# Residual scaling behind tile 0's mixing, late modulation units between the first chunk's steps, and two more projection blocks as three single passes

## The reference, cut to what matters

```python
mod = silu(cvec) @ w_ada + b_ada                  # six rows of 1024, one set for prompt, one for sample
h = rmsnorm(x, g1) * (1.0 + sc1) + sh1
p = h @ w_in                                      # 2832 columns, for three groups of heads
mix = concatenate([fourier_mix(xa), conv_mix(xb), mlstm_mix(xc)])   # 256 + 256 + 512 = 1024 columns
x = x + ga1 * (mix @ w_out)
h = rmsnorm(x, g2) * (1.0 + sc2) + sh2
x = x + ga2 * moe(h, ...)                         # 16 experts in 4 groups, top 2 of one group
y = rmsnorm(x, final_g)
```

## Time and profile before

| | us |
|---|---|
| runs | 1074.56, 1075.64, 1080.11; median 1075.64 |
| the profiled execution | 1078.45, span 1076.5, mean granted clock 0.98 |
| busy: PE / PEld / DVE / ACT / POOL | 1010.8 / 800.5 / 671.7 / 431.6 / 204.2 |

### The profile page before, as it was taken

One profiled execution on the slowest core, in us unless ns is written; L12 is line 12 of the kernel. 1 busy time (PEld: TensorE's weight loads), 2 busy tenths in 40 slices (PEclk: granted clock), 3 DMA queues, 4 the chain that ended last, 5 costly groups with the idle time before them and its releaser, 6 DMA issues.

```text
span 1076.5 us, 18838 instructions
## 1 busy us (share of the span) xinstructions
PE 1010.8 (94%) x6265; PEld 800.5 (74%) x6266; DVE 671.7 (62%) x1121; ACT 431.6 (40%) x875; POOL 204.2 (19%) x240
## 2 busy tenths in 40 slices
PE   6899999989999999999959999988999999989997
PEld 3799999989999987799935666666566665656665
DVE  3444877147698823369955444677576766657677
ACT  3444222254322324679941222212454444344434
POOL 3010000000000001214650000001334433425314
PEclk9999999999999999999988999999999999989999
DMA  9953434313343322142361332257497888887956
GB/s 366 335 184 121 151 118 149 105 60 118 117 142 133 103 73 93 40 131 66 70 255 59 118 118 97 79 181 293 142 318 207 290 261 280 261 290 207 296 158 274
DMA packets 58301, 184.58 MB, mean 171 GB/s; under 512 B 7781, under 2 KB 20711, under 8 KB 52103
## 3 DMA queue, kind: packets, MB, share of 16 engines
q1 hardware_dynamic: 48920, 151.02, 39.5%
q0 software_dynamic: 7632, 27.79, 10.8%
q10 hardware_dynamic: 1696, 5.10, 1.2%
HBM read 149.73 MB, written 34.16 MB: 171 GB/s over the span
## 4 chain that ended last, share of the span: by engine, by line
PE 83%; DVE 5%; DMA 4%; ACT 4%; issue 2%; SPq 1%; POOL 0%; ACTq 0%; POOLq 0%; DVEq 0%
PE psum L1405 43%; PE psum L1347 31%; PE psum L1670 2%; DMA RB<-in_w_exp 1%; PE psum L1271 1%; DMA RW<-h_scratch,idxc 1%; DMA RB<-modrow_scratch 1%; PE psum L1287 1%; PE psum L1362 1%; PE psum L1570 1%; PE psum L1326 1%; DMA gvec<-in_gvec 1%; ACT RE L1152 1%; ACT RA L1162 1%; PE psum L1520 1%
## 5 line engine op out<-in xcount | busy, mean ns | idle before, releaser
L1347 PE MATMUL psum<-input_parts,weight_parts 128*128 128x320 f32 x2208 | 341.0, 313 | 3.0 <-DVE input_parts L1811 3.0
L1347 PEld LDWEIGHTS psum<-input_parts,weight_parts 128*128 128x128 f32 x2208 | 327.2, 190 | 11.8 <-issue 6.9
L1405 PE MATMUL psum<-RB,RW 128*128 x324 | 147.5, 606 | 8.4 <-DMA RB<-in_w_exp 4.8
L954 ACT ACTIVATE weight_parts<-RW 128x1024 fp32r<-128x1024 f32 x46 | 48.7, 1059 | 226.0 <-PE psum L1347 219.4
L1818 DVE TENSOR_TENSOR weight_parts<-RW,weight_parts 128x1024 fp32r<-128x1024 f32 x46 | 56.4, 1225 | 114.9 <-ACT weight_parts L954 114.7
L1405 PE MATMUL psum<-expert_parts 128*128 128x512 f32 x486 | 126.3, 413 | 1.1 <-DVE expert_parts L2343 1.1
L1405 PEld LDWEIGHTS psum<-RB,RW 128*128 128x128 f32 x324 | 60.7, 194 | 76.8 <-issue 76.6
L1405 PEld LDWEIGHTS psum<-expert_parts 128*128 128x128 f32 x486 | 91.3, 188 | 31.6 <-issue 14.3
L762 POOL TENSOR_TENSOR RE<-RE,RA 2x2304 f32<-2x2304 f32 (+1 forms) x2 | 9.1, 4529 | 353.7 <-DMA RA<-in_b_ada 353.6
L1405 PE MATMUL psum<-RC,RB 128*128 128x512 f32 x160 | 74.7, 612 | 0.0
L2362 DVE TENSOR_TENSOR expert_parts<-RB,expert_parts 128x1024 fp32r<-128x1024 f32 x54 | 63.8, 1223 | 9.2 <-ACT expert_parts L1219 8.0
(11 more groups left out here) (385 smaller groups left out, 1576.1 us busy)
## 6 DMA issues: line engine op xcount, KB each, us to landing
RB<-in_w_exp SPq DMA_DIRECT2D x48, 1024.0 KB
RW<-in_w_in SPq DMA_DIRECT2D x46, 512.0 KB, 4.2
RW<-in_w_ada SPq DMA_DIRECT2D x34, 512.0 KB, 3.4
RA<-in_w_ada SPq DMA_DIRECT2D x10, 512.0 KB, 13.9
RW<-gm_scratch SPq DMA_DIRECT2D x20, 256.0 KB, 3.4
h_scratch<-RE SPq DMA_DIRECT2D x10, 512.0 KB, 2.6
acc_scratch<-RA SPq DMA_DIRECT2D x10, 512.0 KB, 3.6
RB<-acc_scratch SPq DMA_DIRECT2D x10, 512.0 KB, 8.3
```

The source lines that it names most:

```text
L954: nc.scalar.activation(spl[:, r, 0], raw[:, r], ACT.Copy).then_inc(whi_ok, 1)
L1347: last = nc.tensor.matmul(psum[:, 2 * r + g, 0:GW], spl[:, r, wv, k], hT[:, xv, k, g * GW:(g + 1) * GW], start=(k == 0 and wv == 0 and xv ...
L1405: return nc.tensor.matmul(out, lhsT, rhs, start=start, stop=stop, **kw_)
```

## The change

Three parts change. `first_ada(2)` is issued ahead of step 1 of chunk 0, `first_ada(3)` ahead of step 2 and both `mod_columns` ahead of step 3; ScalarE copies their rows ahead of evictions 2 and 3. The two scalings of `A2` move behind `mix_tile(0)`, `mix_tile(1)`, the splits and the memsets, right ahead of the loop over tiles. For tiles 4 to 9 (`MORE = 4`) the blocks k 4 and 5 are three single passes too: ScalarE makes `heads_hi` (once) and `headp[..., 0]` (per tile), DVE `heads_lo` (in the place of w_out slices 4 and 5) and `headp[..., 1]`. `half_ps` gets one more count, after block 5 of tile 3, so that the slices are overwritten only when no float32 block needs them.

```diff
@@ -39,6 +39,7 @@
 SK = 2
 WARM = 3
 HK = 4
+MORE = 4
 LATE = 2
 HELD = (7, 9)
 LAG = 2
@@ -75,9 +76,13 @@
     RA = sbuf("RA", [P, 8 * T])
     RS = sbuf("RS", [P, 4 * D])
     RB = sbuf("RB", [P, NSLOT * T])
-    with nc.sbuf_tensor("row_of_slot", [P, LATE * T], F32R) as row_of_slot:
-        owner = row_of_slot[:, :].rearrange("p (b t) -> p b t", b=LATE)
+    with nc.sbuf_tensor("row_of_slot", [P, 5 * D], F32R) as row_of_slot:
+        owner = row_of_slot[:, 0:LATE * T].rearrange("p (b t) -> p b t", b=LATE)
+        heads_lo = row_of_slot[:, 0:2 * D].rearrange("p (k n) -> p k n", k=2)
+        headp = row_of_slot[:, 4 * D:5 * D].rearrange("p (b v k t) -> p b v k t", b=2, v=2, k=2)
     RC = sbuf("RC", [P, NT * NH * (HD + 1)])
+    with nc.sbuf_tensor("heads_weight", [P, 4 * D], F32R) as heads_weight:
+        heads_hi = heads_weight[:, :].rearrange("p (s b n) -> p s b n", s=2, b=2)[:, :, 0]
     RW = sbuf("RW", [P, 4 * D])
     RE = sbuf("RE", [P, 3 * T])
     rows1_ = sbuf("rows1", [P, P])
@@ -261,7 +266,7 @@
     assert mb + 4 * FE <= rb + 2 * D
     G_U = SK * 2 * FE
     D_U = KD * 2 * FE
-    SPLIT0 = 2 * NCH + HK + NT - 1
+    SPLIT0 = 2 * NCH + HK + NT - 1 + 2 + NT - MORE
     yb = RE[:, 0:2 * D].rearrange("p (b c) -> p b c", b=2)
     gmix, gmix_last = RC[:, 4 * D:5 * D], RC[:, LATE * T:LATE * T + D]
     token = RC[:, LATE * T:(LATE + 1) * T]
@@ -444,7 +449,10 @@
     STORED = 32 * (NT // 2)
 
     def mix_split(t):
-        return 2 * NCH + (1 if t == 1 else HK + t)
+        return 2 * NCH + (1 if t == 1 else HK + t if t <= MORE else HK + 2 * t - MORE + 2)
+
+    def heads_split(t):
+        return 2 * NCH + HK + 2 * t - MORE + 3
 
     def wout_split(k):
         return 2 * NCH + 2 + k
@@ -926,9 +934,9 @@
                 g = h * KD + k
                 if h == 0 and k == 0:
                     act.wait_ge(mod_ok, 3)
+                if h == 0 and k in (2, 3):
+                    first_rows(k)
                 if h == 0 and k == KD // 2:
-                    first_rows(2)
-                    first_rows(3)
                     act.wait_ge(mod_ok, 6)
                 act.wait_ge(tr_ps, g + 1)
                 if g >= 2:
@@ -1163,8 +1171,18 @@
                                          accum_out=hss[:, 0, ft, hd:hd + 1]).then_inc(hsq_ok, 1)
         def mix_high(t):
             h, cols = tile_cols(t)
-            act.wait_ge(half_ps, t)
+            act.wait_ge(half_ps, t if t <= MORE else t + 1)
             nc.scalar.activation(mixp[:, 0], PT[:, h, 0:HK, cols], ACT.Copy).then_inc(whi_ok, 1)
+
+        def heads_high(t):
+            h, cols = tile_cols(t)
+            if t == MORE:
+                act.wait_ge(mod_ok, 6 + 2)
+                act.wait_ge(h2_ok, 2 * PT_TILES)
+                for k in range(2):
+                    nc.scalar.activation(heads_hi[:, k], wout(HK + k), ACT.Copy).then_inc(whi_ok, 1)
+            act.wait_ge(mix_ok, NH * t + 2)
+            nc.scalar.activation(headp[:, t % 2, 0], PT[:, h, QQ:QQ + 2, cols], ACT.Copy).then_inc(whi_ok, 1)
 
         act.wait_ge(fn_ok, JOINED)
         act.wait_ge(hn_ok, NT)
@@ -1182,6 +1200,8 @@
                 nc.scalar.activation(score[:, 0:BATCH * NE], psum[:, 6, 0:BATCH * NE], ACT.Sigmoid).then_inc(sig_ok, 1)
             if t + 2 < NT:
                 mix_high(t + 2)
+                if t + 2 >= MORE:
+                    heads_high(t + 2)
             h2_transposed(t)
             logits_part(t)
         act.wait_ge(lg_ps, NT)
@@ -1334,9 +1354,9 @@
                     pe.wait_ge(cm_ev, ev)
                 for k in range(KD):
                     if first:
-                        if h == 0 and k == KD // 2:
-                            first_ada(2)
-                            first_ada(3)
+                        if h == 0 and k in (1, 2):
+                            first_ada(1 + k)
+                        if h == 0 and k == 3:
                             mod_columns(2, 2)
                             mod_columns(3, 2)
                         if k + 2 < KD:
@@ -1618,17 +1638,25 @@
                     pe.wait_ge(mix_ok, NH * (t + 1))
                 if k < HK and t >= 1 and g != 1:
                     pe.wait_ge(wlo_ok, wout_split(k) if t == 1 else mix_split(t))
+                if k == HK and t >= MORE and g != 1:
+                    pe.wait_ge(wlo_ok, heads_split(t))
+                if k < HK and t >= 1:
+                    parts = mixp[:, 0, k], mixp[:, 1, k], wout_hi[:, k], wout_lo[:, k]
+                elif HK <= k < HK + 2 and t >= MORE:
+                    parts = headp[:, t % 2, 0, k - HK], headp[:, t % 2, 1, k - HK], heads_hi[:, k - HK], heads_lo[:, k - HK]
+                else:
+                    parts = None
                 for half in range(2) if g is None else (g,):
                     out, c = psum[:, 2 * (t % 2) + half, :], slice(half * 512, (half + 1) * 512)
-                    if k < HK and t >= 1:
-                        mm(out, mixp[:, 0, k], wout_hi[:, k, c], k == 0, False)
-                        mm(out, mixp[:, 0, k], wout_lo[:, k, c], False, False)
+                    if parts:
+                        mm(out, parts[0], parts[2][:, c], k == 0, False)
+                        mm(out, parts[0], parts[3][:, c], False, False)
                     else:
                         last = mm(out, PT[:, h, MIX[k], cols], wout(k)[:, c], k == 0, k == KD - 1)
-                if k < HK and t >= 1:
+                if parts:
                     for half in range(2) if g is None else (g,):
-                        last = mm(psum[:, 2 * (t % 2) + half, :], mixp[:, 1, k], wout_hi[:, k, half * 512:(half + 1) * 512], False, False)
-                if k == HK - 1 and g is None:
+                        last = mm(psum[:, 2 * (t % 2) + half, :], parts[1], parts[2][:, half * 512:(half + 1) * 512], False, False)
+                if (k == HK - 1 or (k == HK + 1 and t == MORE - 1)) and g is None:
                     last.then_inc(half_ps, 1)
                 if k == KD - 1:
                     last.then_inc(o_ps, 1)
@@ -2099,14 +2127,20 @@
                                         hss[:, 2, ft].unsqueeze(2).broadcast_to([P, NH, HD]), ALU.mult).then_inc(hn_ok, 1)
 
 
-        dve.wait_ge(rows_b, 16 * 7)
-        for q in range(2):
-            nc.vector.scalar_tensor_tensor(A2[:, q], A2[:, q], 1.0, g2row, ALU.add, ALU.mult).then_inc(mod_ok, 1)
-
         def mix_low(t):
             h, cols = tile_cols(t)
             dve.wait_ge(whi_ok, mix_split(t))
             nc.vector.tensor_tensor(mixp[:, 1], PT[:, h, 0:HK, cols], mixp[:, 0].bitcast(F32), ALU.subtract).then_inc(wlo_ok, 1)
+
+        def heads_low(t):
+            h, cols = tile_cols(t)
+            if t == MORE:
+                dve.wait_ge(half_ps, MORE + 1)
+                dve.wait_ge(whi_ok, heads_split(t) - 1)
+                for k in range(2):
+                    nc.vector.tensor_tensor(heads_lo[:, k], wout(HK + k), heads_hi[:, k].bitcast(F32), ALU.subtract).then_inc(wlo_ok, 1)
+            dve.wait_ge(whi_ok, heads_split(t))
+            nc.vector.tensor_tensor(headp[:, t % 2, 1], PT[:, h, QQ:QQ + 2, cols], headp[:, t % 2, 0].bitcast(F32), ALU.subtract).then_inc(wlo_ok, 1)
 
         dve.wait_ge(so_ok, 2)
         mix_tile(0)
@@ -2183,6 +2217,9 @@
         dve.wait_ge(tab_in, 48)
 
 
+        dve.wait_ge(rows_b, 16 * 7)
+        for q in range(2):
+            nc.vector.scalar_tensor_tensor(A2[:, q], A2[:, q], 1.0, g2row, ALU.add, ALU.mult).then_inc(mod_ok, 1)
 
         def normed(t):
             q = 0 if t < PT_TILES else 1
@@ -2223,6 +2260,8 @@
             if t + 2 < NT:
                 mix_tile(t + 2)
                 mix_low(t + 2)
+                if t + 2 >= MORE:
+                    heads_low(t + 2)
             if t == BATCH:
                 dve.wait_ge(sig_ok, 1)
                 choose(0, BATCH, *pairs_a)
```

## The result

| | before | changed |
|---|---|---|
| timed together: median (lowest to highest) | 1076.40 us (1074.56 to 1080.11) | 1059.84 us (1057.69 to 1061.54) |
| ratio | | 0.9841 [0.9808, 0.9873] |
| timed again on another chip | 1080.86 us | 1058.93 us, ratio 0.9808 [0.9756, 0.9861] |
| the profiled execution, span | 1078.45, 1076.5 | 1059.77, 1058.0 |

What follows compares the result with a forecast made beforehand. TensorE was taken to bound the kernel, with 83% of the span in its chain. Gains of 11.5 + 3.3 + 2.6 = 17.4 us off 1078.45 gave 1061.0 profiled, median 1058.2 us; range 1055.0 to 1065.0.

Steps and rivals of the forecast that it cites:

- Part 1: Tile 0: moving the two scalings behind the mixing ends tile 0 11.5 us earlier; bounds 9.3 and 12.0.
- a walk's 12.0: Tile 0: step-by-step timing of TensorE and DVE gave 12.0 us; 11.5 taken, as meeting chains seldom meet exactly.
- The two chains: Tile 0's h2 ready at 574.0, just when TensorE asks for it at 574.0; the scalings' cover is used up.
- The clock: Rival: granted clock falls again in tile 0, the head or both; price 1.3 and 2.2, 1059.5 to 1061.7 us; chance 0.22.
- clock 1.00 through tile 0: Sign that would show the forecast right: granted clock 1.00 through tile 0, where 0.50 was seen before.
- Part 2: Head, chunk 0: late modulation units between the steps gain 3.3 us, 2.0 of it at DVE's modulation; bounds 2.0 and 0.
- 2.0 if the clock falls again: Head, chunk 0: bound on part 2's gain, 2.0 us instead of 3.3 if the clock falls to half again.
- Part 3: Tiles 4 to 9: two more blocks as single passes gain 0.64 us a tile; only tiles 4 to 7 collect, 2.6 us.
- tiles 8 and 9: Forecast: their saving turns into waiting for DVE's routing. Rival: they collect too, 1.3 us better, 1056.9 us; chance 0.09.
- The sum: Whole kernel: 11.5 + 3.3 + 2.6 = 17.4 us off, median 1058.2 us; chance 0.52.

Runs made afterwards that it cites:

- doubled scalings: Changed kernel with two more 128x1024 scalings of the same form queued right behind the two moved ones, 2.36 us more on DVE; ratio 0.9823.
- 22 fillers: Changed kernel with the old order of chunk 0's steps and 22 small unread matmuls, eight between the column matmul groups and 14 behind the second; ratio 0.9864.
- part 3 alone: Kernel before with only blocks 4 and 5 of tiles 4 to 9 as three single passes; ratio 0.9977.
- part 1 alone: Kernel before with only the two scalings moved behind the mixing; 1069.50 us against 1079.75, ratio 0.9912.
- part 2 alone: Kernel before with only the late modulation units and column matmuls moved between the first chunk's steps; ratio 0.9975.
- changed again: The changed kernel unaltered, timed once more on another chip; 1058.93 us against 1080.86, ratio 0.9808.
- tile 3 as well: Changed kernel with tile 3's two projection blocks also as three single passes (MORE = 3); ratio 0.9817.
- old order with fillers among the units: Changed kernel with the old order of chunk 0's steps and 36 small unread matmuls among the late modulation units and between the column matmuls; ratio 0.9893.
- one late unit: Changed kernel with one late modulation unit between steps 0 and 1, the other with the column matmuls back between steps 3 and 4; ratio 0.9855.

## Why the prediction held, step by step

- **Part 1** was forecast at 11.5 of a walk's 12.0, and is 11.8, all of it by itself. The stand is 1.38 us, not 1.15: DVE starts the eviction 0.1 later and TensorE 0.1 after its end. The two chains meet as forecast: TensorE waits 0.16 us for tile 0's h2, and doubling the scalings shows that there is no cover left. Of the 0.5 us that the forecast took off its walk for this meeting, 0.2 is lost ahead of tile 1 and 0.3 in it.
- **The clock**, the rival with the largest chance, did not fall behind the stand for the heads in the changed kernel, in either trace of it. The argument for it was weak: 1.15 us was called less than both stands of the head, and it is more than one of them (1.05), and the stand measured is 1.38. The decision for full clock was right and not well founded. Nor was the sign "clock 1.00 through tile 0" met: behind a stand of 2.40 us, tile 0's first group of 16 ran at the lower level (0.53 and 0.62 in the windows from 544 to 548) as it had before, so this costs nothing against the old kernel. The Trainium skill ("TensorE: Matmul & The Clock Gate", HAM oscillation) says that waits between bursts of matmuls halve the clock. The traces agree there, and behind the 2.43 us of the kernel with doubled scalings; behind the 1.38 us for the heads they show no fall in six of six.
- **Part 2**: forecast 3.3, the traces give 3.18 (48.94 to 45.76), DVE's modulation at 38.43 for 38.5, the unit's last slice 0.24 us late for 0.4. The split: from step 4 to the last step, the same work with short stands on both sides, it is 4.29 us in the changed kernel (41.47 to 45.76) and was 5.43 (43.51 to 48.94). So 1.1 is the clock (forecast 1.3) and 2.0 the order (2.0); the old order under full clock, 4.39 us in this stretch in the kernel with 22 fillers, bears the first out. The bound "2.0 if the clock falls again" was badly put, however: in all five traces with the old stand of 1.69 us before step 4 the clock stood at half in the steps behind it, and in none of the eight with the new order. In the kernel with part 3 alone it had fallen already ahead of the column matmuls, behind a stand of 2.14 us.
- **Part 3**: 0.67 us a tile for the 0.64 forecast, since a pass takes 0.231 us and not 0.233 (8 float32 instructions of 3.44 us in all, less 0.67, over 12 passes). Tiles 4 to 7 collect 2.68 (forecast 2.6), tiles 8 and 9 between 0.2 and 0.3, not 1.3: both the changed kernel and the one with passes in these two alone need 29.5 us from tile 7's residual, against 29.79.
- **The sum**: in the two profiles the changed kernel is ahead by 3.0 us at tile 0's first block, 14.8 at tile 1's first pass, 17.15 at tile 7's residual and 17.4 at tile 9's last half; the spans differ by 18.5. The remaining 1.1 lies behind the tiles, in the experts' part, where nothing was changed. That stretch took between 364.4 and 371.4 us in the fourteen traces, so 1.1 is no more than chance. The parts timed alone give 9.5, 2.7 and 2.5 us (the ratios, of 1079.75 us); each trace's number (11.8, 3.2, 2.7) lies in the interval of its ratio, and only the first part is resolved by times.
- **Luck in the sum.** That 17.4 was forecast and 17.4 measured is in part luck, since the one trace of the kernel before is one of several that the same code gives. The head took 20.65, 21.06 and 23.29 us in the old order (before, part 1 alone, part 3 alone) and 17.06 to 18.24 in eight traces in the new one. From tile 0's first block to tile 1's first pass it took 30.13, 29.64 and 28.16 us with the scalings in the old place (before, part 2 alone, part 3 alone) and 16.89 to 18.98 in eleven traces with them moved. In both places no trace of the old form comes near one of the new, so the gains and their causes are shown, but their sizes only to within some 3 us. Part 3 repeats best: from tile 1's first pass to tile 7's residual 101.62 to 102.00 us in four traces without the passes in these tiles, and 98.95 to 99.33 in six with the passes from tile 4 on (the doubled scalings left out).

## What to carry to other kernels

Before an operation is queued on an in-order engine, ask what its input waits for: two scalings of 2.4 us held their wait of 8 us for a transfer in front of work that was ready. A wait is best filled by real work of the engine that waits, put right behind the instruction whose result travels through the other engines, and here the clock then stayed up at no cost; fillers put where the stand already was came too late. And a local saving ends where another engine's chain begins: give the cheaper form to the tiles in which the engine it relieves is the releaser, and to no others.

## What the runs showed of the hardware

**A stand of 1.4 us never cost the clock in tile 0, longer ones did sometimes.** The stand for the heads was 1.38 us in six traces (changed, changed again, part 1 alone, tile 3 as well, doubled scalings, old order with fillers among the units): the 16 instructions behind it took 7.03 us each time. At 1.63 us (old order with 22 fillers) it was 7.03 too, and at 2.01 to 2.02 us 7.03 in three traces and 8.73 in one. The 16 instructions of tile 0's first blocks, behind a stand of 2.0 to 2.6 us and thin work ahead of it, took 8.7 to 8.8 us in nine traces and 7.13 in two (both behind 2.40); behind 1.38 us, in one trace, they took 7.13. So from 2.0 to 2.4 us the same instructions met half clock in one execution and full clock in another, in kernels that differ elsewhere.

**A part of the spread between runs arises in the first 27 us.** In four traces of fourteen TensorE did the first column matmuls and the modulation unit behind them slower (in a fifth, part of that unit). The first columns of the kernel with fillers among the late units, and of the changed one in its second trace:

```profile
18.35 1.87 PE L1319 MATMUL psum<-gsum,RE 128*128 128x2 f32 x8 [0.72 <-ACT RE L914]
```

```profile
18.09 1.05 PE L1315 MATMUL psum<-gsum,RE 128*128 128x2 f32 x8 [0.73 <-ACT RE L914]
```

The ratio, 1.8, is near that of the two clock levels, and step 0 begins up to 3.8 us later (32.08 against 28.27). Yet the granted clock of that window reads 1.00 (the first of the two kernels):

```profile
18.00:22.00 4.00, 3.65 (x31) 2.57 (x35) 1.76 (x3) 2.37 (x5) 1.95 (x5) 1.00 1.03 410
```

In the fifth trace, of the old order with 22 fillers, column and records agree: 16 matmuls of that unit take 1.03 us where the granted clock reads 0.50 (20 to 23) and 0.62 where it reads 1.00. In the kernel with one late unit the same 16 take 1.03 us under a column of 1.00. So the four slow starts look like the lower level, and why the column does not show it there stays open. Step 0 comes between 27.40 and 32.08 us in the fourteen traces; the stretch behind tile 9 spreads by more, 7.0 us. That is why distances between two rows, such as step 0 to last step, and not absolute times are compared throughout.
